# Hybrid diffusion backbone: how the modulation units are spread over the steps of the A/D attention stage

## The chip, the cores and the metric

One core of one Trainium2 chip runs the whole program. The time is the device time of an execution in microseconds (us); the figure quoted is the median of the runs.

## What is computed

Two trunk layers are run for two groups of tokens that share the weights: 128 context tokens and 512 latent tokens of width 1024. In each layer:

```
mod   = split(silu(cond) @ w_ada + b_ada, 6)       # shift1 scale1 gate1 shift2 scale2 gate2, for both groups
h     = rms_norm(x) * (1 + scale1) + shift1
heads = h @ w_in   -> mixer A: 2-D neighbourhood attention, 4 heads   (softmax over <= 3 blocks of 128 keys)
                      mixer B: multi-scale pooling
                      mixer C: latent attention, 4 heads              (softmax over <= 5 blocks)
                      mixer D: windowed attention with a sink logit   (softmax over <= 4 blocks)
x     = x + gate1 * (concat(A, B, C, D) @ w_out)
x     = x + gate2 * (relu((rms_norm(x) * (1 + scale2) + shift2) @ w1) ** 2 @ w2)
```

The modulation `mod` needs `w_ada`, 1024 x 6144 per layer, which is multiplied with only two condition vectors.

## The kernel before

The five engines run their own programs, written out by hand in the order in which they issue, and wait for one another on semaphores. Nothing is planned at run time: an engine that reaches an unfulfilled wait stops, and all that stands behind it in its program waits too.

**Modulation units.** `w_ada` of a layer is cut into 48 units of 512 x 256 values (512 KB). A unit is one load by SyncE (`load_ada`) and one `ada_tick` on TensorE: eight matmul records that use the array as four strips of 32 columns. Two units (an even one and the odd one behind it) add up in one place of a PSUM bank, four units fill the bank's row of 512 sums. Then ScalarE copies the row to SBUF (`ada_row`; in its `ada_tick` of the fourth unit), TensorE transposes the row in four pieces (the "turn", a tick of its own), and VectorE reduces and adds the bias (`mod`).

The last 16 units of a layer, those of gate1, shift2, scale2, gate2 that are left (`48 * l + 32` and on), are done in and just before the attention of mixers A and D. There are 20 ticks: ticks 4, 9, 14 and 19 are the turns 0 to 3, the others are units 0 to 15 in order (`ONE_BANK`). All of them use bank 6, so unit 4, 8 and 12 wait until VectorE has reduced the turn before. Their loads go to two slots only (`ada_place`: `u % OWN`, `OWN = 2`): the load of unit k is issued when unit k - 2 has been used (`load_ada` waits on `ada_used`). Ticks 0 and 1 stand in front of the attention (`EARLY = 2`).

**The attention of A and D** is one software pipeline of 20 pairs (mixer, query block, two heads), first the 10 of A and then the 10 of D; each mixer begins with its two context pairs, which have one block of 128 keys; a latent pair of A has three, one of D three or four. The pipeline has the lag 3. In step j:

- TensorE: the scores of pair j (it waits until ScalarE is done with the exponentials of pair j - 2), then the step's tick, then the transposes of the probabilities of pair j - 3, then the product with the values of pair j - 4.
- ScalarE: the step's tick (the row copy, after the fourth unit of a row), then `take_turned` of pair j - 3, `take_out` of pair j - 4, then the exponentials of pair j (`exps`).
- VectorE: `take_out` of pair j - 5, the mask and the maximum of pair j (`maxima`), the step's tick (the reduction behind a turn), the reciprocal for pair j - 1.
- GpSimd: the division of pair j by its sum.

Before, step j holds tick j + 2: step 0 unit 2, step 1 unit 3, step 2 turn 0, steps 3 to 6 units 4 to 7, step 7 turn 1, steps 8 to 11 units 8 to 11, step 12 turn 2, steps 13 to 16 units 12 to 15, step 17 turn 3. From step 21 on the first products with `w_out` stand between the steps.

In the trace: L2035 is a unit on TensorE, L2022 a turn, L2189 the scores, L2200 the transposes of probabilities, L2222 the values, L1999 the output projection. On ScalarE L1091 are the exponentials and L899 is the helper that makes all copies (`ada_row`, `pt_a`, `h_hi`). On VectorE L1638 and L1644 add table and mask, L1645 is the maximum, L1647 (A) and L1653 (D) end `maxima`, L1367 and L1369 make `mod`, L1664 is the second part of `take_out`. L733 is a unit's load.

Of the kernel before, what the change touches and what calls it, by code (L numbers as in the profile page):

```python
# [200 lines left out]
def hybrid_kernel(nc, a, o):  # L201
# [150 lines left out]
    with ctx:  # L352
# [269 lines left out]
        def wait_ada(eng, u):  # L622
            eng.wait_ge(ada_dma[ada_place(u)], 16 * (len(ada_before(u)) + 1))

        IN_ATTENTION, EARLY = 20, 2
        LAG = {"C": 2, "AD": 3}

        def late_ticks(l, stage):
# [265 lines left out]
        def _(act):  # L894
# [179 lines left out]
            def attention(l, kind_list, behind_exps={}):  # L1074
                lag = LAG[kind_list]
                todo = [(pair_at[(l, *p)], p) for kind in kind_list for p in attention_pairs(kind)]

                def exps(i, pair):
                    kind = pair[0]
                    act.wait_ge(max_ready, signals(i, 0))  # L1080
                    ring = LAG["C" if kind == "C" else "AD"]
                    if i >= ring:

                        act.wait_ge(turned, i - ring + 1)
                    scale = SCALE_C if kind == "C" else SCALE
                    if kind == "D":

                        do(nc.scalar.activation(sink_e[:, i % 2, :], sink_e[:, i % 2, :], ACT.Exp))
                    for h in range(2):
                        act.wait_ge(max_ready, signals(i, h))  # L1090
                        do(nc.scalar.activation(probs(i, pair)[:, h, :], scores(i, pair)[:, h, :], ACT.Exp,  # L1091
                                                bias=nb[:, i % 2, h:h + 1], scale=scale,
                                                accum_out=lsum[:, i % 3, h:h + 1]),
                           exp_done if h or kind == "C" else None)

                def take_turned(i, pair):

                    act.wait_ge(turned, i + 1)
                    if i >= 2:
                        act.wait_ge(pv_done, i - 1)  # L1100
                    dst, n = probs_t(i, pair), keys_of(pair[0], pair[1])
                    w = min(n, 4) * P
                    src = ps[:, 2048:3072].rearrange("p (h n) -> p h n", h=2)[:, :, 0:w]
                    if n == 5:
                        copy(dst[:, :, 0:w], src)
                        copy(dst[:, :, w:w + P], ps[:, 3072:3072 + 2 * P].rearrange("p (h n) -> p h n", h=2), pt_ready)
                    else:
                        copy(dst[:, :, 0:w], src, pt_ready)

                def take_out(i, pair):  # L1110
                    act.wait_ge(pv_done, i + 1)
                    dst, src = mixed_at(l, pair)
                    copy(dst[0], src, mix_hi)

                for j in range(len(todo) + lag + 1):
                    if kind_list == "AD" and j + EARLY < IN_ATTENTION:
                        ada_tick(48 * l + 32, j + EARLY)
                    if kind_list == "C" and j < len(todo):
                        exps(*todo[j])
                    if j in behind_exps:  # L1120
                        behind_exps[j]()
                    if lag <= j < len(todo) + lag:
                        take_turned(*todo[j - lag])
                    if j >= lag + 1:
                        take_out(*todo[j - lag - 1])
                    if kind_list == "AD" and j < len(todo):
                        exps(*todo[j])
# [198 lines left out]
        def _(dve):  # L1326
# [291 lines left out]
            def attention(l, kind_list):  # L1618
                lag = LAG[kind_list]
                todo = [(pair_at[(l, *p)], p) for kind in kind_list for p in attention_pairs(kind)]  # L1620

                def maximum_c(i, pair, h):

                    dve.wait_ge(scored, signals(i, h))
                    do(V.tensor_reduce(mx[:, i % 2, h:h + 1], scores(i, pair)[:, h, :], AX_X, ALU.max))
                    do(V.tensor_scalar(nb[:, i % 2, h:h + 1], mx[:, i % 2, h:h + 1], -SCALE_C, None, ALU.mult), max_ready)

                def maxima(i, pair):

                    kind, b, hp = pair  # L1630
                    s = scores(i, pair)
                    dve.wait_ge(scored, signals(i))
                    if kind == "A" and b is not None:
                        if b:
                            dve.wait_ge(table_ready, 3 * l + b)
                        v = s[:, :, 0:256]
                        table = a_table[b][:, 2 * hp:2 * hp + 2, :, :].rearrange("p h r c -> p h (r c)")
                        do(V.tensor_tensor(v, v, table, ALU.add))  # L1638
                    if kind == "D" and b is not None:
                        lo = max(b - 1, 0)  # L1640
                        for blk, m in ((b - 1, 0), (b + 1, 1)):
                            if 0 <= blk < 4:
                                v = s[:, :, P * (blk - lo):P * (blk - lo) + P]
                                do(V.tensor_tensor(v, v, band[:, m, :].unsqueeze(1).broadcast_to([P, 2, P]), ALU.add))  # L1644
                    do(V.tensor_reduce(mx[:, i % 2, :], s, AX_X, ALU.max))  # L1645
                    if kind == "A":
                        do(V.tensor_scalar(nb[:, i % 2, :], mx[:, i % 2, :], -SCALE, None, ALU.mult), max_ready)  # L1647
                    else:

                        sink = gains[:, GAIN_AT["swa_sink"] + hp:GAIN_AT["swa_sink"] + 4:2]  # L1650
                        do(V.scalar_tensor_tensor(mx[:, i % 2, :], mx[:, i % 2, :], SCALE, sink, ALU.mult, ALU.max))
                        do(V.tensor_scalar(nb[:, i % 2, :], mx[:, i % 2, :], -1.0, None, ALU.mult))
                        do(V.tensor_tensor(sink_e[:, i % 2, :], sink, mx[:, i % 2, :], ALU.subtract), max_ready)  # L1653

                def reciprocals(i, pair):
                    dve.wait_ge(exp_done, signals(i))
                    if pair[0] == "D":
                        do(V.tensor_tensor(lsum[:, i % 3, :], lsum[:, i % 3, :], sink_e[:, i % 2, :], ALU.add))
                    do(V.reciprocal(rinv[:, i % 3, :], lsum[:, i % 3, :]), rinv_ready)

                def take_out(i, pair):
                    dve.wait_ge(mix_hi, i + 1)
                    dst, src = mixed_at(l, pair)
                    do(V.tensor_tensor(dst[1], src, f32(dst[0]), ALU.subtract), mix_lo)  # L1664

                for j in range(len(todo) + lag + 2):
                    if kind_list == "C":
                        if 1 <= j < len(todo) + 1:
                            reciprocals(*todo[j - 1])
                        if j < len(todo):  # L1670
                            maximum_c(*todo[j], 0)
                        if j >= lag + 2:
                            take_out(*todo[j - lag - 2])
                        if j < len(todo):
                            maximum_c(*todo[j], 1)
                        continue
                    if j >= lag + 2:
                        take_out(*todo[j - lag - 2])
                    if j < len(todo):
                        maxima(*todo[j])  # L1680
                    if j + EARLY < IN_ATTENTION:
                        ada_tick(48 * l + 32, j + EARLY)
                    if 1 <= j < len(todo) + 1:
                        reciprocals(*todo[j - 1])

# [27 lines left out]
            for l in range(DEPTH):  # L1713
# [60 lines left out]
                for d in range(KC):  # L1774
                    j = d // 2
# [169 lines left out]
        def _(pe):  # L1945
# [95 lines left out]
            def ada_ticks(first, ks):  # L2041
                for k in ks:
                    ada_tick(first, k)
# [106 lines left out]
            def attention(l, kind_list, before_turn):  # L2150
# [75 lines left out]
                for j in range(len(todo) + lag + 1):  # L2226
                    if j < len(todo):
                        score(*todo[j])
                    if kind_list == "AD" and j + EARLY < IN_ATTENTION:
                        ada_tick(48 * l + 32, j + EARLY)  # L2230
                    if j in before_turn:
                        before_turn[j]()
                    if lag <= j < len(todo) + lag:
                        turn(*todo[j - lag])
                    if j >= lag + 1:
                        values(*todo[j - lag - 1])
# [16 lines left out]
            for l in range(DEPTH):  # L2253
# [238 lines left out]
                for n in range(first + PLAIN, first + MLP_UNITS):  # L2492
                    u = units[n]
                    g, j = u[2], u[3]
# [86 lines left out]
```

## Time and profile before

| | |
|---|---|
| time, median of 3 runs | 1608.32 us (1606.68 to 1609.83) |
| span of the profiled execution, first to last instruction | 1600.7 us |
| granted TensorE clock, mean | 0.992 |
| TensorE busy | 1541.7 us (96%) |
| VectorE busy | 1085.4 us (68%) |
| ScalarE busy | 846.0 us (53%) |
| GpSimd busy | 118.1 us (7%) |

The profiled execution is given by its span; what lies around the span is not in the trace, and the median of the runs stands 7.6 us above the span. TensorE's matmul ends are modelled, and neighbouring records overlap a little, so spacings are read from start to start. The A/D attention of layer 0 begins near 250 us and that of layer 1 near 1034 us.

### The profile page before, as it was taken

What the parts mean: (1) busy time and instruction counts of PE and PEld (TensorE: products, weight loads), DVE (VectorE), ACT (ScalarE), POOL (GpSimd) and SP (SyncE); (2) the same over time, 40 slices, a digit from 0 to 9 for tenths busy, and PEclk for the clock granted to TensorE, in tenths of its full rate; (3) what the DMA queues carried; (4) which work ended last, traced back from release to release, by engine and by line L of the source; (5) the groups of instructions that cost most, each with busy time, mean ns of one, the idle gap of its engine ahead of it and who ended that gap; (6) DMA issues with size and microseconds to landing.
All of it is one profiled execution on the core that took longest, in us unless ns stands there. A gap on an engine that the chain in (4) does not pass through costs nothing.

```text
span 1600.7 us, 30051 instructions
## 1 busy us (share of the span) xinstructions
PE 1541.7 (96%) x11642; PEld 1439.9 (90%) x11642; DVE 1085.4 (68%) x1951; ACT 846.0 (53%) x1485; POOL 118.1 (7%) x83
## 2 busy tenths in 40 slices
PE   6989999999999999999998999999999999999998
PEld 4867996799999999999976789868999999999998
DVE  5564356677787878787567443584968787878763
ACT  5566536766554545454455564486755454545442
POOL 1004005300000000000000220242000000000000
PEclk9999999999999999999999999999999999999999
DMA  9820544221222222222746024350212222222222
GB/s 331 269 91 2 102 122 144 69 80 53 80 80 80 80 80 80 80 80 80 253 142 212 28 26 129 119 163 28 80 53 80 80 79 81 78 82 77 86 73 67
DMA packets 150581, 160.00 MB, mean 100 GB/s; under 512 B 16358, under 2 KB 132776, under 8 KB 150440
## 3 DMA queue, kind: packets, MB, share of 16 engines
q1 hardware_dynamic: 149736, 157.87, 32.5%
q8 instruction: 93, 1.52, 0.4%
q14 instruction: 48, 0.39, 0.1%
q10 hardware_dynamic: 576, 0.16, 0.0%
q0 software_dynamic: 128, 0.05, 0.0%
HBM read 153.15 MB, written 4.65 MB: 99 GB/s over the span
## 4 chain that ended last, share of the span: by engine, by line
PE 84%; DVE 5%; ACT 5%; DMA 2%; issue 2%; SPq 1%; ACTq 0%; DVEq 0%
PE ps L1999 34%; PE ps L2435 21%; PE ps L2143 13%; PE ps L2451 4%; PE ps L2169 2%; PE ps L2200 2%; PE ps L2222 2%; PE ps L2115 2%; PE ps L2035 1%; PE ps L1978 1%; ACT w_hi L899 1%; DVE extrema L1645 1%; SPq L733 1%; PE ps L2189 1%; DMA ada_own<-in_w_ada 1%
## 5 line engine op out<-in xcount | busy, mean ns | idle before, releaser
L899 ACT ACTIVATE w_hi<-w_raw 128x512 fp32r<-128x512 f32 (+1 forms) x242 | 189.1, 781 | 194.0 <-PE ps L1999 99.6
L2435 PE MATMUL ps<-x_hi,w_hi 128*128 128x322 f32 x784 | 244.3, 312 | 0.6 <-DVE us L1826 0.6
L2435 PE MATMUL ps<-x_hi,w_lo 128*128 128x322 f32 x784 | 243.5, 311 | 0.0
L2435 PE MATMUL ps<-x_lo,w_hi 128*128 128x322 f32 x784 | 243.4, 310 | 0.0
L1999 PE MATMUL ps<-z_hi,w_hi 128*128 128x384 f32 (+1 forms) x1024 | 233.7, 309 | 0.0
L1999 PE MATMUL ps<-z_hi,w_lo 128*128 128x384 f32 (+1 forms) x1024 | 233.1, 309 | 0.0
L1999 PE MATMUL ps<-z_lo,w_hi 128*128 128x384 f32 (+1 forms) x1024 | 233.1, 309 | 0.0
L1346 DVE TENSOR_TENSOR w_lo<-w_raw,w_hi 128x512 fp32r<-128x512 f32 x212 | 146.7, 692 | 36.3 <-ACT w_hi L899 28.0
L2143 PE MATMUL ps<-w_hi,h_hi 128*128 128x256 f32 (+1 forms) x560 | 161.2, 288 | 2.6 <-ACT st L899 1.7
L2143 PE MATMUL ps<-w_hi,h_lo 128*128 128x256 f32 (+1 forms) x560 | 158.0, 282 | 0.0
L2143 PE MATMUL ps<-w_lo,h_hi 128*128 128x256 f32 (+1 forms) x560 | 157.9, 282 | 0.0
L1999 PEld LDWEIGHTS ps<-z_hi,w_hi 128*128 128x128 f32 x1024 | 157.2, 188 | 0.0
L1999 PEld LDWEIGHTS ps<-z_hi,w_lo 128*128 128x128 f32 x1024 | 156.2, 188 | 0.0
L1999 PEld LDWEIGHTS ps<-z_lo,w_hi 128*128 128x128 f32 x1024 | 156.2, 188 | 0.0
L2435 PEld LDWEIGHTS ps<-x_hi,w_hi 128*128 128x128 f32 x784 | 148.0, 189 | 1.1 <-DVE us L1826 1.1
L2435 PEld LDWEIGHTS ps<-x_lo,w_hi 128*128 128x128 f32 x784 | 148.4, 189 | 0.0
L2435 PEld LDWEIGHTS ps<-x_hi,w_lo 128*128 128x128 f32 x784 | 147.6, 188 | 0.0
L899 ACT ACTIVATE w_hi<-w_sum 128x512 fp32r<-128x512 f32 x112 | 70.8, 632 | 136.5 <-PE ps L1999 67.7
L1339 DVE TENSOR_TENSOR w_lo<-w_raw,w_hi 128x2048 fp32r<-128x2048 f32 (+1 forms) x30 | 65.6, 2185 | 78.5 <-ACT w_hi L899 77.9
L1690 DVE SCALAR_TENSOR_TENSOR xT<-ps,mod,xT 128x128 f32<-128x128 f32 x144 | 50.5, 351 | 97.2 <-PE ps L1999 94.3
L2143 PEld LDWEIGHTS ps<-w_hi,h_hi 128*128 128x128 f32 x560 | 107.6, 192 | 5.9 <-issue 3.1
L1692 DVE SCALAR_TENSOR_TENSOR xT<-ps,mod,xT 128x512 f32<-128x512 f32 x144 | 108.2, 751 | 5.1
(291 smaller groups left out, 2853.5 us busy)
## 6 DMA issues: line engine op xcount, KB each, us to landing
w_raw<-in_mlp_w SPq DMA_DIRECT2D x64, 1024.0 KB, 5.4
ada_own<-in_w_ada SPq DMA_DIRECT2D x50, 512.0 KB, 4.5
w_raw<-in_w_in SPq DMA_DIRECT2D x14, 1024.0 KB, 7.8
ada_room<-in_w_ada SPq DMA_DIRECT2D x23, 512.0 KB, 8.7
ada_mix<-in_w_ada SPq DMA_DIRECT2D x17, 512.0 KB, 7.7
w_raw<-in_w_out SPq DMA_DIRECT2D x8, 768.0 KB, 5.3
ada_first<-in_w_ada SPq DMA_DIRECT2D x6, 512.0 KB, 9.0
x_in<-in_x_sample SPq DMA_DIRECT2D x1, 2048.0 KB, 8.5
```

What stands on the lines that cost most here:

```text
L899: do(nc.scalar.activation(out, in_, ACT.Copy), sem)
L1339: do(V.tensor_tensor(w_lo[:, n % 2, 0:w], w_raw[:, n % 2, 0:w], f32(w_hi[:, n % 2, 0:w]), ALU.subtract), w_lo_ready)
L1346: do(V.tensor_tensor(ring_block(w_lo, n, b), block_source(n, b), f32(ring_block(w_hi, n, b)), ALU.subtract), w_lo_ready)
L1690: do(V.scalar_tensor_tensor(x, ctx_part, gate[:, 0:1], x, ALU.mult, ALU.add))
L1692: do(V.scalar_tensor_tensor(x, lat_part, gate[:, 1:2], x, ALU.mult, ALU.add), sem)
L1999: ins = M.matmul(part, lhs, rhs[:, cols], start=first and n == 0, stop=last and n == 2)
L2115: last = M.matmul(bank(CQ_BANKS[t])[:, 0:UW], x[:, k, tok], w[r][:, k, :], start=k == 0 and q == 0, stop=k == KC - 1 and q == 2)
L2143: last = M.matmul(bank(proj_bank(i))[:, 0:cols], x[p][:, k, :], w[r][:, k, :], start=k == 0 and q == 0, stop=k == kk - 1 and q == 2)
L2169: last = M.matmul(out[:, h, c:c + int(np.prod(rhs.shape[1:]))], c_q[0:QK, head, q], rhs, start=True, stop=True, skip_group_check=True)
L2200: last = M.transpose(ps[:, c:c + P], probs(i, pair)[:, h, P * j:P * j + P], ident[:, :])
L2435: last = M.matmul(bank(b, XW), w[r][:, k, :], x_of(x, x_name)[:, k, :], start=k == 0 and q == 0 and not more, stop=k == 3 and q == 2, skip ...
L2451: last = M.matmul(bank(2 * row + half, width), w[r][:, k, :], v, start=k == 0 and q == 0, stop=k == KC - 1 and q == 2)
```

## The change

The ticks are no longer spread one to a step: seven steps take two units each, the four turns have a step to themselves, and seven steps have no tick. That makes 11 of the first 18 steps with ticks. All three engines that have ticks follow the same table. Ticks 0 and 1 stay where they were, and so do the turns (steps 2, 7, 12, 17). Nothing is added to or taken from the work of any engine.

```
-        IN_ATTENTION, EARLY = 20, 2
+        EARLY = 2
+        AD_TICKS = {0: (2, 3), 2: (4,), 3: (5, 6), 5: (7, 8), 7: (9,), 8: (10, 11), 10: (12, 13), 12: (14,),
+                    13: (15, 16), 15: (17, 18), 17: (19,)}
...
# ScalarE
-                    if kind_list == "AD" and j + EARLY < IN_ATTENTION:
-                        ada_tick(48 * l + 32, j + EARLY)
+                    if kind_list == "AD":
+                        ada_ticks(48 * l + 32, AD_TICKS.get(j, ()))
...
# VectorE
-                    if j + EARLY < IN_ATTENTION:
-                        ada_tick(48 * l + 32, j + EARLY)
+                    ada_ticks(48 * l + 32, AD_TICKS.get(j, ()))
...
# TensorE
-                    if kind_list == "AD" and j + EARLY < IN_ATTENTION:
-                        ada_tick(48 * l + 32, j + EARLY)
+                    if kind_list == "AD":
+                        ada_ticks(48 * l + 32, AD_TICKS.get(j, ()))
```

`ada_ticks(first, ks)` calls `ada_tick(first, k)` for each k. By units:

| step | 0 | 1 | 2 | 3 | 4 | 5 | 6 | 7 | 8 | 9 | 10 | 11 | 12 | 13 | 14 | 15 | 16 | 17 |
|---|---|---|---|---|---|---|---|---|---|---|---|---|---|---|---|---|---|---|
| before | 2 | 3 | turn 0 | 4 | 5 | 6 | 7 | turn 1 | 8 | 9 | 10 | 11 | turn 2 | 12 | 13 | 14 | 15 | turn 3 |
| after | 2, 3 | - | turn 0 | 4, 5 | - | 6, 7 | - | turn 1 | 8, 9 | - | 10, 11 | - | turn 2 | 12, 13 | - | 14, 15 | - | turn 3 |

ScalarE's row copies, which stand with units 3, 7, 11 and 15, move from steps 1, 6, 11 and 16 to steps 0, 5, 10 and 15.

## Rows read from the trace of the kernel before

**Rows 1.** The chain that ended last, 245 to 330 us: start us, us, engine, line

```profile
249.51 3.55 DMA ada_own<-in_w_ada
253.11 0.68 PE ps L2035 x8
...
280.39 0.61 ACT ada_row L899
...
283.04 0.97 DVE extrema L1645
```

**Rows 2.** TensorE in order of time, layer 0 (start us, us, what, idle before)

```profile
250.30 0.64 PE L2035 MATMUL ps<-ada_own,cond 128*32 128x256 f32 x8
250.87 0.49 PE L2189 MATMUL ps<-a_k,a_q 64*128 64x128 f32 x4
253.11 0.68 PE L2035 MATMUL ps<-ada_own,cond 128*32 128x256 f32 x8 [1.75 <-DMA ada_own<-in_w_ada]
253.72 1.65 PE L2189 MATMUL ps<-a_k,a_q 64*128 64x256 f32 x8
...
257.75 0.64 PE L2035 MATMUL ps<-ada_own,cond 128*32 128x256 f32 x8 [0.18 <-DVE mod L1367]
...
261.48 0.92 PE L2189 MATMUL ps<-a_k,a_q 64*128 64x256 f32 x8 [0.32 <-ACT pr_a L1091]
...
267.11 0.92 PE L2189 MATMUL ps<-a_k,a_q 64*128 64x256 f32 x8
```

**Rows 3.** ScalarE in order of time, layer 0, steps 0, 1, 3 and 9

```profile
253.89 0.60 ACT L899 ACTIVATE ada_row<-ps 128x512 f32<-128x512 f32 x1 [1.36 <-issue]
254.52 0.37 ACT L1091 ACTIVATE pr_a<-ps,extrema 128x128 f32<-128x128 f32 x1
...
260.05 0.58 ACT L1091 ACTIVATE pr_a<-ps,extrema 128x384 f32<-128x384 f32 x1 [0.76 <-DVE extrema L1647]
...
275.43 0.81 ACT L899 ACTIVATE pt_a<-ps 128x768 f32<-128x768 f32 x1 [0.51 <-ACT pr_a L1091]
```

**Rows 4.** VectorE in order of time, layer 0, steps 2 and 12

```profile
255.49 0.70 DVE L1638 TENSOR_TENSOR ps<-ps,a_table 128x512 f32<-128x512 f32 x1 [2.69 <-PE ps L2189]
...
257.42 0.19 DVE L1367 TENSOR_REDUCE mod<-ps 128x8 f32<-128x32 f32 x1
...
282.25 0.29 DVE L1664 TENSOR_TENSOR h_lo<-ps,h_hi 128x128 fp32r<-128x128 f32 x1 [1.08 <-ACT h_hi L899]
```

**Rows 5.** TensorE in order of time, layer 1, steps 1 to 7

```profile
1037.14 0.64 PE L2035 MATMUL ps<-ada_own,cond 128*32 128x256 f32 x8 [1.69 <-DMA ada_own<-in_w_ada]
1037.70 0.92 PE L2189 MATMUL ps<-a_k,a_q 64*128 64x256 f32 x8
...
1041.19 1.04 PE L2035 MATMUL ps<-ada_own,cond 128*32 128x256 f32 x8
...
1044.81 0.92 PE L2189 MATMUL ps<-a_k,a_q 64*128 64x256 f32 x8
...
1048.84 0.64 PE L2035 MATMUL ps<-ada_own,cond 128*32 128x256 f32 x8 [0.26 <-DMA ada_own<-in_w_ada]
...
1051.02 0.92 PE L2189 MATMUL ps<-a_k,a_q 64*128 64x256 f32 x8
```

**Rows 6.** Windows of 2 us: window, length, busy (x) of each engine, clock, DMA, GB/s

```profile
254.00:256.00 2.00, 2.00 (x11) 1.61 (x12) 0.51 (x1) 1.40 (x5) 0.00 (x0) 0.50 0.65 204
...
1040.00:1042.00 2.00, 2.00 (x16) 1.05 (x14) 1.76 (x6) 1.21 (x4) 0.59 (x1) 0.50 0.46 158
```

**Rows 7.** TensorE, layer 0, near 21 and 73 us: units side by side

```profile
20.93 1.93 PE L2035 MATMUL ps<-ada_first,cond 128*32 128x256 f32 x32 [1.04 <-DVE xT L1698]
22.80 1.60 PE L2066 MATMUL ps<-ident,few 128*128 128x128 f32 x12
```

**Rows 8.** Loads into `ada_own`, 240 to 310 us: issue to landing, 14 loads

```profile
DMA to landing us min/median/max: 3.4/4.4/4.7
```

**Rows 9.** Part 6 of the page: KB each, median us from issue to landing

```profile
w_raw<-in_mlp_w SPq DMA_DIRECT2D x64, 1024.0 KB, 5.4
```

## What the change is predicted to do

> **What bounds the kernel now.** I read the page first: TensorE is busy 96% of the span, and the change neither adds nor removes work. So the question is only what the new order does to the waits inside the two A/D stages, about 70 us each. The chain of waits comes second, because it says which engine's delay reaches the end. In layer 0 it enters the stage through a load: unit 3 is released by its own DMA, issued at 249.51 and landed 3.55 us later. Then come TensorE pieces up to 278, ScalarE with a row copy and the copy behind it from 280.39, and from 283.04 on VectorE's maxima [rows 1]. The timelines then give the spacing of single steps.
>
> Three facts carry the argument. First, unit 3 cannot start before 253.11, whichever step it stands in: its slot comes free with unit 1, and TensorE idles 1.75 us for the landing [rows 2]. Second, between score 5 and step 9 TensorE is the bound (after the 0.32 us wait at 261.48 the timeline shows it none), so what delays it there stays. Third, from step 12 VectorE works without a gap, and its start there (282.25) waits for ScalarE's `take_out` [rows 4], which descends through a saturated ScalarE from the copy at 275.43, held 0.51 us by TensorE's transposes [rows 3]. A delay of TensorE up to step 9 is therefore handed to ScalarE and from there to the end of the stage. What TensorE saves after step 9 is not.
>
> **Start of the stage, layer 0 (steps 0 to 5).** Before, ScalarE does the exponentials of pair 0 while TensorE waits for unit 3, and only the copy of the row (253.89, 0.60 us) and the exponentials of pair 1 come behind it. After, the copy stands in step 0, ahead of the exponentials of pair 0, and score 1 stands behind unit 3.
>
> - The copy still starts at 253.89. The exponentials of pair 0 take the place that pair 1's have now: start 254.52; each of the two is 0.37 and a read of the accumulator behind it, some 0.95 us together, so they end near 255.46 [rows 3].
> - Score 2 waits for exactly these. It starts near 255.55 instead of 253.72 [rows 2]. Score 2 is then cold as now: at 254 to 256 the granted clock is 0.50, the 1.2 GHz level, after TensorE's idle time in front of unit 3 [rows 6]; with 1.65 us it ends at about 257.15, against 255.37 now: +1.75. What is late next is VectorE, which waits for that score (255.49, idle 2.69) and reaches the reduction of turn 0 at 257.42 [rows 4]: both +1.7.
> - Unit 4 waits for that reduction (0.18 us already now, 257.75 [rows 2]): +1.7. The exponentials of pair 3 (260.05, released by VectorE [rows 3]) move by the same 1.7, and score 5 (261.48) waits for them: **+1.7 at score 5**. Leaving unit 5 out of step 4 brings nothing there, since score 5 waits for ScalarE, and now waits about 0.8 instead of 0.32.
>
> **Start, layer 1.** The same landing (1037.14), but the clock falls a little later against the work: now score 2 (1037.70) runs warm in 0.92, score 3 runs cold, and unit 4 costs 1.04 instead of 0.64 [rows 5]; 1040 to 1042 is at 0.50 [rows 6]. After, score 2 starts near 1039.55, runs cold for 1.65 and ends near 1041.2, +2.6 on 1038.6; VectorE's maximum of pair 2 (about 1.8 us, as from 255.49 to 257.42 [rows 4]) brings unit 4 to 1043.45, +2.25 on 1041.19, now at full clock. Score 5 comes at **+2.3**.
>
> **The pairs.** Four units side by side take 22.80 - 20.93 = 1.87 us [rows 7]; a lone one takes 0.57 from its start to the next instruction's (250.30 to 250.87 [rows 2]). So each further neighbour costs (1.87 - 0.57) / 3 = 0.43, and a pair saves 0.14. Seven pairs in two layers: 1.9 us of TensorE time. What counts is only where TensorE is the bound: the pair 6, 7, 0.13 in each layer. The pair in step 3 is hidden by score 5's wait; that of step 8 by ScalarE, which gets the transposes of pair 5 0.43 later and then has no 0.51 us of idle time left at 275.43 [rows 3]; those of steps 10, 13 and 15 by ScalarE and VectorE. If none were hidden they would give -1.9; nothing in the rows lets them cost time. The row copies moved from steps 11 and 16 to 10 and 15 still cost 0.6 each on ScalarE on the same path, once: 0.
>
> By the Trainium skill ("TensorEngine Tiling (Array Packing)", Key Properties), changing the tiling mode drains TensorE. Rows 7 agree as to sign, and put the price at 0.14 us for a pair; by the rule alone the change is a gain, and it is the faster rival below.
>
> **Loads two at a time.** With two slots, the loads of units 6 and 7 now leave within about 0.45 us of each other, behind units 4 and 5. Now they leave 2 us apart and a load lands in 3.4 to 4.7 us [rows 8]. No row has two 512 KB loads of this kind at once. From below: the second still lands in 4.7 at most, some 5.15 after the first is issued. From above: one load of the joint size, 1024 KB, takes 5.4 [rows 9], and sharing could add a little. Against that stands the time to the use: from the end of unit 4 to score 5 is 263.2 - 259.95 = 3.25, then 0.85 for the score and 0.43 for unit 6, so unit 7 is wanted 4.5 after the first issue. The stall is 0.65 to 0.9, or nothing if both came as fast as the fastest one (3.4 + 0.45 = 3.85). I take 0.8 in layer 0 and 0.85 in layer 1, by the 1024 KB row, which is nearest. In layer 1 short waits of this kind exist already, the longest 0.26 us before unit 7 [rows 5], and they go. Later pairs have more time: three steps (5 to 8, 10 to 13), or two of three-block steps (8 to 10, about 4.9 us up to unit 11; 13 to 15), where a short stall falls into TensorE's slack behind step 9.
>
> By the Trainium skill ("DMA: Bandwidth & Descriptors", Anatomy of one DMA) a transfer costs about 2.0 us and its bytes over 436 GB/s; for a pair that is some 4.4 us, an estimate, and unit 7 would hardly wait. Its figures are for GpSimd's path. By them the change costs about 1.6 us less than in my sum. The 5.4 us row speaks against it here.
>
> **Sum.** From score 5 to score 7 is 5.63 us in layer 0 now [rows 2]; after, it is 5.63 - 0.13 + 0.8. Score 7: 1.7 - 0.13 + 0.8 = +2.4. In layer 1 (1051.02 - 1044.81 = 6.21 now, 0.58 more than in layer 0, the short waits and what hangs on them [rows 5]): 2.3 - 0.13 - 0.58 + 0.85 = +2.45. From there TensorE, ScalarE and VectorE in turn hand it on unchanged. Together +4.85 us on the span of 1600.7, so about 1605.5, and with the 7.6 us by which the median stands above the span, **1613.2 us**, 0.3% slower. Less than 0.2%, about 3.2 us, cannot be told from no change.
>
> **Rivals.**
>
> - *The pair of loads lands in time.* Unit 7 does not wait; the start alone remains: 1.6 + 1.6 = +3.2 us, 1611.5. For it: 3.4 us landings exist. Against: those had the queue for themselves. Chance 0.17.
> - *A second stretch at 1.2 GHz.* In steps 1 and 2 TensorE is idle about 3 us after the change, where it was idle some 2 now. If the clock rises only after unit 5, turn 0, score 3 and two units cost about twice: some 1.4 to 2 us more on TensorE. The 0.8 us that it would wait before score 5 hides part of that; 0.6 to 1.7 a layer are left, so 1614.5 to 1616.5. Against: TensorE is busy in most of the cold stretch (score 1, score 2). Chance 0.13.
> - *The packing wins: not slower.* If the start's delay is taken up before step 12 by idle time of ScalarE in steps 5 to 9 (0.51 us at 275.43 [rows 3]) and of VectorE (1.08 at 282.25 [rows 4]), and TensorE's savings of 0.14 count in each pair, the time is 1608.3 - 1.9 = 1606.4. It decides if the chain is carried by TensorE's total work in the stage instead of by its order, from the first step in which ScalarE waits for transposes (step 5) on. For it: TensorE is busy 96% and the stage is nearly full. Against: just then the delay is one of TensorE itself, the two idle times are ones that it causes, and nothing shortens its queue by more than 0.14 a pair. If in addition the moved copies took ScalarE off the path (0.6 us in each of steps 11 and 16), it would be 1604. Chance 0.17, two in five of it faster by over 0.2%.
>
> The forecast itself has 0.53. Its own range is 1611 to 1615.5. Over all cases I give 1608.6 to 1616.6. Slower by over 0.2%: all but a tenth of the forecast's and the second stretch's 0.66 and half of the first rival's, so 0.69; faster 0.08; same 0.23.
>
> **What would show it.** In the profile after: unit 3 directly behind unit 2, still starting near 253.1 and 1037.1; score 1 behind it and an idle wait of score 2 for ScalarE's exponentials, score 2 near 255.6 and 1039.6; the row copy ahead of pair 0's exponentials; a wait for `ada_own`'s DMA before unit 7 in step 5; pairs of 16 records in 1.05 us busy; score 7 near 269.5 and 1053.5; VectorE still without a gap from step 12. The prediction is wrong if score 2 starts near its old time, if unit 7 has no wait, or if score 12 is late by less than 1 us while VectorE's chain starts on time.

## The result: 0.6% slower, by more than forecast

The changed kernel takes 1615.2 us (median of 6 runs, 1612.61 to 1619.6) against 1607.24 us for the kernel before (6 runs, 1604.08 to 1609.83). The ratio is 1.0061, 95% interval 1.0043 to 1.008: some 10 us slower (7 to 13); the medians lie 8.0 us apart. The forecast was 1613.2 us, or +4.9. The sign was right, and so were the two places that were named, the stage's start and step 5; the size was half of what was measured.

The profiled execution of the changed kernel has a span of 1617.8 us, 17.1 more than that of before, and is the longest of its runs. The profile of before comes from a short execution: in every run whose own span is known the time stands about 2 us above it, so this one took some 1602.7 us (an estimate), less than any of the six timed. Most of the 7.6 us in the prediction's sum is this distance. So the two profiles must be cut into stretches first. From the first score of the A/D attention (step 0) to the first product of the output projection (step 21), start to start on TensorE:

| | layer 0 | layer 1 | both against before |
|---|---|---|---|
| before | 60.12 | 59.93 | |
| after | 63.12 | 65.15 | +8.2 |

The stretch behind it, to the first product with `w1`, takes 62.8 us in both layers of both kernels. The stages' 8.2 us are not given back. The other 8.9 us of the two profiles' distance lie in code that is the same in both: +2.8 before the first stage, +7.5 between the stages, -1.4 at the end. The mean granted clock, 0.992 and 0.983, makes some 26 and 55 us at 1.2 GHz (an estimate: the span times twice the clock's distance from 1); the stages have 7 and 14 of them, the rest lies elsewhere. No part of the 8.9 us is put down to the change, because the code there is the same; that is an argument, and no run shows it. The stages' 8.2 us agree with the measured 8 to 10. Each is one execution; what repeats is seen in the first experiment, whose order from score 5 on is that of before: 48.8 and 48.6 us to the output projection, against 48.5 and 49.1.

The page of the changed kernel, head and first lines: work is as before, TensorE is "busy" for 10 us more because some of it ran at half the clock.

```profile
span 1617.8 us, 30053 instructions
PE 1552.0 (96%) x11642; PEld 1449.2 (90%) x11642; DVE 1086.5 (67%) x1951; ACT 846.1 (52%) x1485; POOL 118.1 (7%) x83
```

TensorE in order of time, layer 0, steps 0 to 7, the answer to [rows 2]:

```profile
252.70 0.49 PE L2190 MATMUL ps<-a_k,a_q 64*128 64x128 f32 x4 [0.43 <-DVE h_lo L1769]
253.12 0.64 PE L2036 MATMUL ps<-ada_own,cond 128*32 128x256 f32 x8
255.97 0.64 PE L2036 MATMUL ps<-ada_own,cond 128*32 128x256 f32 x8 [2.21 <-DMA ada_own<-in_w_ada]
256.54 0.68 PE L2190 MATMUL ps<-a_k,a_q 64*128 64x128 f32 x4
258.45 1.65 PE L2190 MATMUL ps<-a_k,a_q 64*128 64x256 f32 x8 [1.22 <-ACT pr_a L1093]
260.03 1.11 PE L2023 MATMUL ps<-ident,ada_row 128*128 128x128 f32 x4
261.07 1.65 PE L2190 MATMUL ps<-a_k,a_q 64*128 64x256 f32 x8
262.65 1.48 PE L2036 MATMUL ps<-ada_own,cond 128*32 128x256 f32 x16
...
266.43 0.92 PE L2190 MATMUL ps<-a_k,a_q 64*128 64x256 f32 x8 [0.34 <-ACT pr_a L1093]
267.36 0.64 PE L2036 MATMUL ps<-ada_own,cond 128*32 128x256 f32 x8
268.79 0.64 PE L2036 MATMUL ps<-ada_own,cond 128*32 128x256 f32 x8 [0.79 <-DMA ada_own<-in_w_ada]
...
273.00 0.92 PE L2190 MATMUL ps<-a_k,a_q 64*128 64x256 f32 x8
```

Read it from score 0. Score 2 comes at +5.75 us (before: +3.84) and waits for ScalarE's exponentials, which it did not before. It, turn 0 and score 3 run at half speed, and so does the first part of the pair 4, 5 (1.48 us, at full clock 1.07). Unit 7 waits 0.79 us for its load. Score 5 is 2.1 us later than before, score 7 3.1.

ScalarE in the same steps, the answer to [rows 3]: the row copy now comes first, and the exponentials of pair 0 (the two at 257.45 and 257.94) behind it.

```profile
256.82 0.60 ACT L901 ACTIVATE ada_row<-ps 128x512 f32<-128x512 f32 x1 [4.22 <-PE ps L2036]
257.45 0.37 ACT L1093 ACTIVATE pr_a<-ps,extrema 128x128 f32<-128x128 f32 x1
257.94 0.37 ACT L1093 ACTIVATE pr_a<-ps,extrema 128x128 f32<-128x128 f32 x1
```

The granted clock in windows of 2 us, the answer to [rows 6] (the value behind GpSimd's busy time):

```profile
256.00:258.00 2.00, 1.23 (x12) 0.52 (x12) 0.59 (x2) 1.12 (x4) 0.00 (x0) 0.68 0.76 238
258.00:260.00 2.00, 1.55 (x8) 1.18 (x8) 0.17 (x1) 1.31 (x6) 0.61 (x1) 0.50 0.68 221
260.00:262.00 2.00, 2.00 (x10) 1.56 (x10) 1.72 (x3) 0.00 (x0) 0.00 (x0) 0.50 0.07 23
262.00:264.00 2.00, 2.00 (x22) 0.88 (x19) 1.76 (x6) 1.35 (x4) 0.61 (x1) 0.62 0.00 0
```

Summed over the windows at a stage's start, the kernel before spends 3.4 us at 1.2 GHz in each layer; this one spends 6.8.

TensorE in layer 1, steps 2, 3, 5 and 10, the answer to [rows 5], and the loads issued in two small windows there (slots of `ada_own`, two loads in the first, one in the second):

```profile
1053.10 1.65 PE L2190 MATMUL ps<-a_k,a_q 64*128 64x256 f32 x8 [1.41 <-ACT pr_a L1093]
...
1057.31 1.80 PE L2036 MATMUL ps<-ada_own,cond 128*32 128x256 f32 x16
...
1061.41 0.92 PE L2190 MATMUL ps<-a_k,a_q 64*128 64x256 f32 x8 [0.34 <-ACT pr_a L1093]
1062.26 0.64 PE L2036 MATMUL ps<-ada_own,cond 128*32 128x256 f32 x8
1064.20 0.64 PE L2036 MATMUL ps<-ada_own,cond 128*32 128x256 f32 x8 [1.30 <-DMA ada_own<-in_w_ada]
...
1078.15 0.64 PE L2036 MATMUL ps<-ada_own,cond 128*32 128x256 f32 x8 [0.36 <-DMA ada_own<-in_w_ada]
1079.52 0.64 PE L2036 MATMUL ps<-ada_own,cond 128*32 128x256 f32 x8 [0.73 <-DMA ada_own<-in_w_ada]
```

```profile
DMA to landing us min/median/max: 5.2/5.7/6.1
...
DMA to landing us min/median/max: 5.0/5.0/5.0
```

The first of these answers is for the loads of units 10 and 11 (issued at 1072.9 and 1073.3), the second for that of unit 7 (1059.2). In the kernel before no load of either layer's stage took more than 4.7 ([rows 8] for layer 0).

The account of the 8.2 us, each as the distance from score 0, after minus before:

| | layer 0 | layer 1 | sum | forecast |
|---|---|---|---|---|
| up to score 5 | +2.1 | +3.3 | +5.4 | +4.0 |
| score 5 to score 7 | +0.95 | +0.8 | +1.75 | +0.85 |
| score 7 to the output projection | -0.05 | +1.1 | +1.05 | 0 |

### The profile page after: what moved, and what is told of

Read it like the earlier page. It is cut to its first block, busy times and chain, and to the rows that moved or that the text cites. A ratio compares the mean times of both kernels' runs of the same rounds, so it can differ in the third digit from the quotient of the medians.

```text
span 1617.8 us, 30053 instructions
## 1 busy us (share of the span) xinstructions
PE 1552.0 (96%) x11642; PEld 1449.2 (90%) x11642; DVE 1086.5 (67%) x1951; ACT 846.1 (52%) x1485; POOL 118.1 (7%) x83
## 4 chain that ended last, share of the span: by engine, by line
PE 85%; DVE 5%; ACT 5%; DMA 3%; issue 2%; ACTq 0%; SPq 0%; DVEq 0%
PE ps L2000 33%; PE ps L2436 21%; PE ps L2144 13%; PE ps L2452 4%; PE ps L2170 2%; PE ps L2036 2%; PE ps L2201 2%; PE ps L2223 2%; PE ps L2116 2%; PE ps L1979 2%; DMA ada_own<-in_w_ada 1%; ACT w_hi L901 1%; DVE extrema L1647 1%; PE ps L2190 1%; DMA ada_mix<-in_w_ada 1%
```

## The experiments

Every experiment is a form of the changed kernel; e6 and e10 have its table set back to one tick to a step, as before. The first line of each gives the ratio to the kernel before, timed on the same chip, with its interval, and the stages' extra length in the profile, layer 0 and layer 1 together, against before. A profile is one execution; its stage lengths carry that execution's landings and clock.

**Only the first pair (e1).** The table is `{0: (2, 3)}`, then one tick to a step.

> Only units 2 and 3 are paired in step 0; all other ticks stand one to a step as before. Theory (delay at the start): ScalarE's row copy gets ahead of the exponentials of pair 0, score 2 comes 1.9 us later, score 5 about 2 us later than before in each layer, no wait for a load in step 5: 3.5 to 4.5 us above before. Rival (the start is absorbed, the later pairs' loads cost all): within 1 us of before.

Ratio 1.0035 (1.0021 to 1.0049), +5.6 us; stages +5.4. Score 5 is 1.9 and 3.7 us later than before, 6.8 and 10.2 us are spent at 1.2 GHz. The start by itself costs more than half of the change. The expectation (3.5 to 4.5 us) had no more time at the lower clock than before; the stages lie above it, and the interval of the time (3.4 to 8.2 us) reaches down to it.

**All pairs but the first (e2).**

```
{0: (2,), 1: (3,), 2: (4,), 3: (5, 6), 5: (7, 8), 7: (9,), 8: (10, 11), ...}
```

> Units 2 and 3 stay in steps 0 and 1, the six later pairs are as in the change. Theory (loads two at a time): unit 7 waits 0.8 to 1.3 us for its load in step 5, in some layers units 10 or 11 too; the start is as before: 2 to 3.5 us above before. Rival (all of the cost is at the start): within 1 us of before, or 1 to 2 us below it by the packing of units.

Ratio 1.0003 (0.9992 to 1.0014); stages +3.8. The two answers differ: the profiled execution has the waits for loads (unit 7: 0.54 and 1.73 us; units 10 and 11 in layer 1: 0.68 and 0.73; unit 15: 1.14), the timed runs show at most 2.3 us. In layer 1 of this execution the clock did not fall at all. The waits are real, but their size differs from one execution to the next, and by the times alone this part would be the smaller one. Unit 15's wait, in step 15, costs nothing: from score 7 to the output projection layer 0 takes 42.8 us, as before (42.9). The two waits in step 10 of layer 1 cost all of their 1.4 us there (44.3 against 42.9). TensorE in layer 1, step 5, the longest of them:

```profile
1048.84 0.64 PE L2036 MATMUL ps<-ada_own,cond 128*32 128x256 f32 x8
1051.21 0.64 PE L2036 MATMUL ps<-ada_own,cond 128*32 128x256 f32 x8 [1.73 <-DMA ada_own<-in_w_ada]
```

**ScalarE's copy in step 1 (e3).** TensorE's order stays that of the change.

```
-                        ada_ticks(48 * l + 32, AD_TICKS.get(j, ()))          # ScalarE
+                        ada_ticks(48 * l + 32, {0: (2,), 1: (3,)}.get(j, AD_TICKS.get(j, ())))
```

> The changed kernel, but ScalarE copies the first row in step 1, behind the exponentials of pair 0; TensorE's order is that of the change. Theory (the copy ahead of the exponentials is what makes score 2 late): score 2 starts about 0.5 us behind score 1 instead of 1.9 us; some 1.3 us a layer come back, 2.5 to 3 us below the changed kernel. Rival (the late score 1 on TensorE is what costs): no more than 0.5 us below the changed kernel.

Ratio 1.0023 (1.0011 to 1.0035), 6 us below the changed kernel. Scores 1 and 2 run as one (12 records, started at 253.31), and score 5 is 1.4 us earlier in both layers, which is what the copy's place is worth there:

```profile
252.41 0.97 PE L2036 MATMUL ps<-ada_own,cond 128*32 128x256 f32 x8 [2.17 <-DMA ada_own<-in_w_ada]
253.31 2.08 PE L2190 MATMUL ps<-a_k,a_q 64*128 64x128 f32 x12
```

Score 5 still stands 0.7 and 1.9 us behind the kernel before, and the stages are still +6.1. Layer 1 of this execution spent 6.8 us at 1.2 GHz at the stage's start, although the copy stood behind the exponentials, and 3.4 more after waits of 0.89 and 0.73 us for units 6 and 7. So moving the copy alone does not always keep the longer slow time away (layer 0 has 3.4 us). The times give back more than the expected 2.5 to 3 us and more than the stages show (2.1); the distance between two ratios has an interval of some 3.5 us either way.

**Half-size loads (e4).** Units 4 to 15 load 256 KB.

```
+                rows = 2 if u % 48 >= 36 else 4
+                src = a["w_ada"][u // 48, k:k + 128 * rows, c:c + AC]
```

> The changed kernel with the loads of units 4 to 15 of these steps cut to half (256 KB; the other half of the slot keeps old values, so the modulation is not the reference's). Theory (two loads at once reach TensorE late): no wait before unit 7 in step 5 nor before units 10 and 11; 2 to 3.5 us below the changed kernel. Rival (the waits only stand in for something else in step 5): the same time as the changed kernel within 0.7 us.

Ratio 1.0024 (1.0009 to 1.0039); stages +6.2. The waits before units 7, 10 and 11 are gone in both layers. A load takes 3.0 us (layer 0, median), and the pair 6, 7 is one group:

```profile
266.13 1.07 PE L2038 MATMUL ps<-ada_own,cond 128*32 128x256 f32 x16
```

From score 5 to score 7 it takes 5.66 and 5.79 us, where the changed kernel takes 6.57 and 7.01: the waits are worth 0.9 and 1.2 there. That the stages are at +6.2 all the same lies at the start: score 5 stands 0.6 us later in either layer than in the changed kernel, and layer 1 spends 10.2 us at 1.2 GHz.

**Extra matmuls in the idle time (e5, then e9 with the right size).**

```
+    def filler(n): n times M.matmul(bank(7)[:, P:2 * P], ident, ident)
+    ... in front of unit 3: filler(15), in step 1: filler(8)      # e9: 9 and 4
```

> The changed kernel with 15 extra 128x128 matmuls on TensorE in front of unit 3 and 8 in step 1, in its idle time there, into columns that nobody reads. Theory (half of the start's cost is the stretch at the lower clock): the granted clock stays at 1.0 in steps 1 to 5, score 5 comes 1 to 1.5 us earlier in each layer than in the changed kernel, 2 to 3 us in all. Rival (the order of ScalarE alone sets it, the slow stretch is covered): score 5 at the same distance from score 0 within 0.3 us, the same time.

Ratio 1.0058 (1.0036 to 1.0079); stages +9.8. A filler takes 0.24 us, so fifteen of them don't fit into 2.2 us of idle time; unit 3 started 1.3 us late, and the run says only that 23 of them keep the clock at 1.0.

> The changed kernel with 9 extra matmuls in front of unit 3 and 4 in step 1, sized by their measured 0.24 us each so that they fit into the idle time (the earlier fillers held unit 3 up by 1.3 us). Theory (the slow stretch costs besides the copy's delay): clock 1.0 throughout the stage's start, score 5 near 12.7 us behind score 0 instead of 13.7 and 14.2; 1 to 3 us below the changed kernel. Rival (waits for ScalarE and VectorE cover the slow stretch): score 5 stays at 13.5 or more.

Ratio 1.0027 (1.0013 to 1.004), 5.5 us below the changed kernel; stages +5.4, of which 1.8 are waits for the loads of units 10 and 11 in layer 0. Unit 3 is on time (+3.23 from score 0), score 2 waits for the same exponentials as in the changed kernel (+5.70, before it +5.75), and from there everything is at full clock:

```profile
252.17 0.64 PE L2043 MATMUL ps<-ada_own,cond 128*32 128x256 f32 x8
252.74 0.49 PE L2197 MATMUL ps<-a_k,a_q 64*128 64x128 f32 x4
253.16 1.16 PE L2016 MATMUL ps<-ident 128*128 128x128 f32 x8
254.64 0.92 PE L2197 MATMUL ps<-a_k,a_q 64*128 64x256 f32 x8 [0.33 <-ACT pr_a L1093]
255.50 0.66 PE L2028 MATMUL ps<-ident,ada_row 128*128 128x128 f32 x4
256.08 0.92 PE L2197 MATMUL ps<-a_k,a_q 64*128 64x256 f32 x8
257.95 1.07 PE L2043 MATMUL ps<-ada_own,cond 128*32 128x256 f32 x16 [0.94 <-DVE mod L1369]
...
261.68 0.92 PE L2197 MATMUL ps<-a_k,a_q 64*128 64x256 f32 x8 [0.70 <-ACT pr_a L1093]
```

Score 5 stands at 12.7 and 12.8, against 13.7 and 14.2. So the slow stretches cost 1.0 and 1.3 us before score 5. The row with 0.94 shows why it is not more: at full clock the units wait for VectorE instead. The 5.5 us by the times are more than the 1 to 3 expected, and their interval is as wide as above.

**The same in the kernel before (e6, then e10).**

> The kernel before with 12 extra matmuls in front of unit 3. Theory: its one slow stretch at the stage's start goes, score 5 comes about 1 us earlier in each layer, 1.5 to 2.5 us below before. Rival (the stretch is covered by waits in the kernel before): the same time within 0.5 us.

Ratio 0.9981 (0.9969 to 0.9994), with unit 3 held up 1.1 us by its 12 fillers and stages 1.6 us longer than before. In layer 0 unit 7 waited 0.78 us for its load, which took 5.3 us although the load before it had left 2 us earlier. The twelve runs are faster than the kernel before, and the one profile has longer stages; this stays unexplained.

> The kernel before with 6 extra matmuls in front of unit 3, 1.45 us in 1.75 us of idle time. Theory: clock 1.0, unit 3 not held up, score 5 near 10.5 us behind score 0 in both layers instead of 11.6 and 10.8; 1 to 2 us below before. Rival: score 5 unchanged, the same time within 0.5 us.

Ratio 1.0003 (0.9989 to 1.0018). The clock stays at 1.0, score 5 is 0.6 us earlier in layer 0 and no earlier in layer 1; stages -0.9 in all. The single slow stretch of the kernel before is nearly covered. My expectation was too high.

```profile
250.97 0.49 PE L2197 MATMUL ps<-a_k,a_q 64*128 64x128 f32 x4 [0.43 <-DVE h_lo L1769]
...
261.93 0.92 PE L2197 MATMUL ps<-a_k,a_q 64*128 64x256 f32 x8 [0.32 <-ACT pr_a L1093]
```

This run and e9 are the two orders with the clock at 1.0 throughout the start, and their difference is the order alone: score 5 at 10.96 and 10.88 here, at 12.74 and 12.83 there, +1.8 and +1.95, 3.7 us in all. The slow stretches make 2.3 us in the changed kernel and 0.6 in the kernel before, so the change adds 1.7 by the clock. Together that is the +5.4 up to score 5.

**Pairs three steps apart (e11).**

```
{0: (2,), 1: (3,), 2: (4,), 3: (5, 6), 6: (7, 8), 8: (9,), 9: (10, 11), 12: (12, 13), 14: (14,), 15: (15, 16), ...}
```

> Units 2 and 3 alone as before, the six later pairs three steps apart (steps 3, 6, 9, 12, 15, 18; turns in 2, 8, 14, 20). Theory (a pair costs only by the distance to the pair before it): no wait for a load before units 5 to 15, stage length as before or up to 0.5 us shorter, 0 to 1 us below before. Rival (pairs cost by themselves, by holding back the transposes of their step): 1 to 3 us above before.

Ratio 1.0004 (0.9989 to 1.0018); stages +1.35. Of all pairs only the first, in step 3, waits for a load (0.87 us, layer 1: unit 5's slot comes free with unit 3, two steps earlier); waits for VectorE's reduction behind a turn come in (0.5 us before unit 4, 1.0 before unit 12). Pairs three steps apart show no cost outside the interval (some 2 to 3 us) and bring nothing; the expected gain of up to 1 us did not come.

**Copy in step 1 and half loads together (e12).** Both edits above.

> The changed kernel with ScalarE's first row copy in step 1 and the loads of units 4 to 15 cut to half (256 KB, the rest of the slot keeps old values, so the modulation is not the reference's). Theory (copy and loads are the two causes, the slow stretch hangs on the first): of the 8.2 us by which the two stages are longer in the profile, 1.5 us at most are left, 0 to 2 us above before in time. Rival (something else in the pairing costs): 3 us or more are left.

Ratio 1.0003 (0.9986 to 1.0019); stages +0.45 of the changed kernel's +8.2. The slow stretch is back to one in each layer (3.4 us at 1.2 GHz), as before the change. With these two mended no cost of the pairing is left that could be told from nothing. Inside the stages two parts cancel: score 5 is still 0.7 us later than before in each layer, and score 5 to score 7 takes 5.49 us in both, against 5.63 and 6.21. The small loads also take away the short waits that the kernel before itself has in layer 1; the kernel before with half loads was not run, so the zero of this comparison is not known to better than some 0.6 us.

**Unit 3 behind score 2 (e7), and units thinned out where TensorE is the bound (e8).**

```
e7  {0: (2,), 2: (3,), 3: (4,), 4: (5,), 5: (6,), ... one to a step ... 18: (19,)}
e8  {0: (2,), 2: (3,), 3: (4,), 5: (5,), 7: (6,), 9: (7,), 10: (8,), 11: (9,), ... one to a step ... 21: (19,)}
```

> One tick to a step as before, but unit 3 stands behind score 2 and all later ticks are one step later (turns in steps 3, 8, 13, 18). Theory (the wait for unit 3's load costs the stage through what stands behind it): TensorE does score 2 while the load lands, score 2 comes about 1 us earlier than before and the idle time is too short for a slow stretch: 2 to 4 us below before. Rival (the stage is bound by total work, the wait moves to another place): the same as before within 1 us.

Ratio 0.9988 (0.9973 to 1.0003), an interval that includes no change; stages -2.9. Score 2 stands at +2.71 from score 0, 1.1 us before its old place, and the load of unit 3 lands behind it; the clock never falls:

```profile
256.29 0.92 PE L2190 MATMUL ps<-a_k,a_q 64*128 64x256 f32 x8 [1.22 <-ACT pr_a L1093]
257.14 0.64 PE L2036 MATMUL ps<-ada_own,cond 128*32 128x256 f32 x8
```

> Unit 3 behind score 2 as in the run before it, and the ticks thinned out in steps 4 to 9 (turn 0 in 3, units 4 to 6 in 5, 7, 9) and one to a step from 10 to 21. Theory (TensorE is the bound up to step 9, VectorE from step 12): three ticks of 0.57 us leave TensorE's part, 1 to 1.5 us a layer, and cost nothing later but one more reduction of 0.4 us on VectorE: 1 to 2.5 us below the run with unit 3 in step 2. Rival (ScalarE bounds steps 5 to 9 as closely): no gain, or 0.5 to 1 us slower by the added reduction.

Ratio 0.9975 (0.9962 to 0.9988), 4 us faster than the kernel before and the fastest of all that was run, 1601.23 us in the median; stages -4.5. Score 8 comes 17.45 us behind score 0, against 20.13 before. One wait is new, for VectorE's reduction before unit 12, in the part where TensorE has time:

```profile
295.44 0.64 PE L2036 MATMUL ps<-ada_own,cond 128*32 128x256 f32 x8 [0.76 <-DVE mod L1369]
```

## Why the prediction had the sign right and half of the size

The forecast had +4.85 us in the stages, the profile has +8.2. Of the 3.4 us between them 1.4 come before score 5, 0.9 between score 5 and score 7, and 1.05 in step 10 of layer 1. The three paragraphs in quotation marks below take them in this order.

**Unit 3 does not move (right).** It starts 2.85 us behind unit 2, before 2.81: its load alone decides.

**The copy ahead of pair 0's exponentials (right).** Score 2 was forecast 1.83 us later against score 0 in layer 0 and came 1.9 later; 2.1 in layer 1 (forecast 1.85). e3 takes the copy back and gets 1.4 us at score 5 in each layer. At full clock the order costs 3.7 us at score 5 (e9 against e10), where the forecast had 1.7 + 2.3 with one slow stretch in it.

**"Score 2 is then cold as now" (the step that failed).** The sum let the clock fall once, as in [rows 6], and return when score 2 ended; the second stretch stood among the rivals, with a chance of 0.13 and 0.6 to 1.7 us a layer. It came in both layers, in the changed kernel and in every other run that has score 1 behind unit 3 and pair 0's exponentials behind the copy, unless fillers kept TensorE busy (e1 and e4 had even more in layer 1, 10.2 us). It came once with the copy moved as well, in layer 1 of e3, and stayed away in layer 0 of e3 and in both layers of e12; what decides between 3.4 and 6.8 us there was not isolated. I argued that TensorE is busy in most of the cold stretch; the windows show 1.23 and 1.55 busy us of 2 where it falls and holds on. Score 5 came at +2.1 and +3.3 instead of +1.7 and +2.3. The forecast and this rival were treated as exclusive where one is a consequence of the other: the longer idle time was my own result.

**"The stall is 0.65 to 0.9" (right in kind, mis-sized).** Unit 7 waited 0.79 and 1.30 us. The forecast timed the loads from units 4 and 5 at full clock and gave the second one 2.8 us before score 5 (3.25 - 0.43). These units ran at half clock in large part (1.48 and 1.80 us for both), and the second load left 2.2 us before score 5 in both layers. It took 4.5 us in layer 0 and 5.0 in layer 1, where I had 4.7 to 4.95 from its own issue. So the 0.79 of layer 0 is luck in part: the load was wanted sooner than forecast and landed sooner too. In layer 1 it landed late, and the wait is longer by the same half microsecond. Unit 6 of layer 1, which waited before, no longer does, as forecast.

Not all of the wait is owed to the pairing. With one unit to a step unit 7 waited too, 0.16 us in e1, 0.40 in e7 and 0.78 in e6, each in one layer.

**"A short stall falls into TensorE's slack behind step 9" (wrong in layer 1).** In layer 0 the pair 10, 11 did not wait. In layer 1 both loads were slow, 5.2 and 6.1 us, the two waits add to 1.1 us, and the stage ended 1.1 us later. Step 10 has no slack: the waits for loads there, 1.1 us here, 1.4 in e2 (layer 1), 1.8 in e9 (layer 0) and 0.9 and 1.7 in e5, lengthened the way from score 7 to the output projection by 1.1, 1.4, 1.8, 0.7 and 1.7 us. The slack begins further on: waits of 1.14 us (e2, layer 0) and 1.16 us (e5, layer 1) in step 15 lengthened it by nothing. Why these two loads took as long was not settled: other runs wait in step 10 too (e2 in layer 1, e9 in layer 0 with 1.10 and 0.73 us), now in one layer and now in the other.

**The packing (right).** A pair is 1.07 us busy and 1.00 from start to start, against 1.14 for two lone units. With loads and copy mended (e12), seven such pairs a layer give nothing that can be seen beyond the 0.13 a layer of the forecast (score 5 to score 7 of layer 0 takes 5.49 us, before 5.63): the stages are +0.45, not -1.9. The rival in which the packing wins is excluded.

**The rest of the profile.** VectorE still works without a gap from step 12 on, after a wait for ScalarE's `take_out` (0.97 and 0.55 us at steps 11 and 12 in layer 0, 2.09 and 0.63 in layer 1), and hands on what it gets.

Taken together, the pair in step 0 makes 5.4 of 8.2 us: 3.7 by the order (the copy ahead of the exponentials, and score 1 behind unit 3) and 1.7 by the clock. The waits for loads make 2.8. e1, which has the first part alone, has +5.4 in the stages; e4, without the waits, has +6.2. How much of the loads' part the typical run pays stays open: e2's times put it at 0 to 2 us, the profiles at 2 to 3.8, and the distance between e4's ratio and the changed kernel's at 5.9, with some 2.5 to 3 us of interval on either ratio. Taken by the ratios, removing the copy's delay (6.1) and removing the waits (5.9) add up to more than the whole 9.8; the intervals allow it, and e4 shows no less time at 1.2 GHz than the changed kernel, so the profiles don't explain it.

## What to carry to other kernels

When work moves to an earlier step of a software pipeline, follow it on every engine that has a share in it. Here unit 3 itself started no later, and the copy that belongs to it got in front of the one instruction on ScalarE for which the next score waits. Then ask what the new idle time does to TensorE's clock, and cost every stretch behind it at both levels. Then look at the loads: with units in pairs, unit 7's load in layer 0 left 0.4 us behind the one before it, not 2.1, and had 3.8 us until it was wanted, not 4.4. And ask in which step a wait falls: in step 10 it cost its whole length, in step 15 nothing.

## What was not expected of the hardware

- Fillers: a 128x128 matmul of this type is two records, 0.24 us in all at full clock; 13 of them in idle time (e9) kept the granted clock at 1.0 and brought the changed kernel from 1.0061 to 1.0027.
- Two loads of 512 KB issued 0.4 us apart took 3.5 and 4.6 us when all went well (layer 0, units 10 and 11), and 5.2 and 6.1 in layer 1. In the kernel before no load of either stage took more than 4.7, but in e6 a single one, issued 2 us behind the load before it, took 5.3.
- In layer 1 of the kernel before the clock fell at this place, in e2 and e11, with the same order up to there and the same idle time (1.7 us), it did not. The same instructions can meet either level from one execution to the next, and that goes for the rest of the program too: the parts that no experiment touched differ by up to 8.9 us between two profiles (from the output projection of layer 0 to score 0 of layer 1: 722.5 us in e5, 731.4 in the changed kernel).
